# Moving the low part of two normed inputs by 64 bytes, the bias matmul to the third panel, and adding a narrow matmul: a float32 transformer kernel on one core

## What is computed

```
for i in range(2):
    h = h + mixer(rmsnorm(h, mix_norm[i]))          # layer 0: stick-breaking + hgrn2; layer 1: sliding window
    h = h + conv_glu_ffn(rmsnorm(h, ffn_norm[i]))   # up: 1024 -> 2 x 2816, 3-tap convolution, silu(gate)*up, down
    h = h + sigmoid(rmsnorm(h, ple_norm[i]) @ ple_gate[i]) * (p[i] @ ple_proj[i])
x = second_block(h, mem, ...)                       # three gated branches, an output matrix, a last norm
```

## Time and profile before

| | |
|---|---|
| median of 3 runs | 1003.98 us (1003.67 to 1004.08) |
| profiled execution, its own time | 1004.01 us |
| its span | 1002.1 us |
| granted clock of the PE | 1.0 in the whole span |
| PE busy | 984.9 us (98%) |
| PE weight loads busy | 883.2 us (88%) |
| DVE, ACT, POOL busy | 677.7, 573.5, 133.8 us |
| HBM read | 172.25 MB |

### The profile page before, as it was taken

One profiled execution on the slowest core, in us unless ns is written; L12 is line 12 of the kernel. 1 busy time (PEld: TensorE's weight loads), 2 busy tenths in 40 slices (PEclk: granted clock), 3 DMA queues, 4 the chain that ended last, 5 costly groups with the idle time before them and its releaser, 6 DMA issues.

```text
span 1002.1 us, 15515 instructions
## 1 busy us (share of the span) xinstructions
PE 984.9 (98%) x6218; PEld 883.2 (88%) x6218; DVE 677.7 (68%) x969; ACT 573.5 (57%) x801; POOL 133.8 (13%) x116
## 2 busy tenths in 40 slices
PE   8999999999999999999999999999999999999997
PEld 8998889999988888788999998888988889988886
DVE  5787577888864567886788886456564566854555
ACT  7747747656553576785756655356464465534433
POOL 4003202343310000000143331001000000000010
PEclk9999999999999999999999999999999999999999
DMA  9654256686555464336766655546635544466551
GB/s 310 207 170 126 84 146 178 197 250 195 185 195 184 167 210 168 126 103 171 198 172 182 194 172 203 177 166 205 211 127 169 168 149 146 142 197 205 175 172 56
DMA packets 159655, 174.33 MB, mean 174 GB/s; under 512 B 4126, under 2 KB 120336, under 8 KB 159584
## 3 DMA queue, kind: packets, MB, share of 16 engines
q1 hardware_dynamic: 157248, 167.65, 53.3%
q0 software_dynamic: 2160, 5.41, 1.7%
q10 hardware_dynamic: 176, 0.27, 0.1%
HBM read 172.25 MB, written 1.07 MB: 173 GB/s over the span
## 4 chain that ended last, share of the span: by engine, by line
PE 85%; ACT 6%; DVE 5%; issue 2%; DMA 1%; POOL 0%; POOLq 0%; ACTq 0%; DVEq 0%
PE bank L870 32%; PE bank L845 29%; PE bank L902 16%; PE bank L890 2%; ACT w_hi L1215 2%; PE bank L1004 1%; PE bank L930 1%; DVE w_lo L1541 1%; DMA w_raw<-in_ab_w_in 1%; ACT le L1325 1%; ACT L1325 1%; PE bank L950 0%; PE bank L973 0%; DVE le_s L1891 0%; ACT le_s L1465 0%
## 5 line engine op out<-in xcount | busy, mean ns | idle before, releaser
L1541 DVE TENSOR_TENSOR w_lo<-w_raw,w_hi 128x2048 fp32r<-128x2048 f32 x154 | 351.9, 2288 | 186.8 <-ACT w_hi L1215 186.6
L1215 ACT ACTIVATE w_hi<-w_raw 128x2048 fp32r<-128x2048 f32 x155 | 296.2, 1914 | 247.5 <-PE bank L870 114.2
L870 PE MATMUL bank<-x_hi,w_hi 128*128 128x256 f32 x720 | 205.9, 286 | 2.7 <-DVE w_lo L1541 1.8
L870 PE MATMUL bank<-x_lo,w_hi 128*128 128x256 f32 x720 | 203.7, 283 | 0.0
L870 PE MATMUL bank<-x_hi,w_lo 128*128 128x256 f32 x720 | 203.7, 283 | 0.0
L870 PEld LDWEIGHTS bank<-x_hi,w_hi 128*128 128x128 f32 x720 | 138.0, 192 | 4.4 <-DVE w_lo L1541 2.0
L845 PE MATMUL bank<-w_hi,x_hi 128*128 128x512 f32 x352 | 139.8, 397 | 1.0 <-DVE x_lo L1555 0.7
L870 PEld LDWEIGHTS bank<-x_lo,w_hi 128*128 128x128 f32 x720 | 138.1, 192 | 0.2
L870 PEld LDWEIGHTS bank<-x_hi,w_lo 128*128 128x128 f32 x720 | 138.0, 192 | 0.0
L845 PE MATMUL bank<-w_hi,x_lo 128*128 128x512 f32 x352 | 137.3, 390 | 0.0
L845 PE MATMUL bank<-w_lo,x_hi 128*128 128x512 f32 x352 | 137.1, 390 | 0.0
(11 more groups left out here) (344 smaller groups left out, 1471.6 us busy)
## 6 DMA issues: line engine op xcount, KB each, us to landing
w_raw<-in_ffn_up SPq DMA_DIRECT2D x88, 512.0 KB, 5.2
w_raw<-in_w_in SPq DMA_DIRECT2D x35, 1024.0 KB, 5.1
w_raw<-in_ffn_down SPq DMA_DIRECT2D x22, 1024.0 KB, 5.0
w_raw<-in_ab_w_in SPq DMA_DIRECT2D x13, 1024.0 KB, 5.4
w_raw<-in_ple_gate SPq DMA_DIRECT2D x8, 1024.0 KB, 5.1
w_raw<-in_c_w_in SPq DMA_DIRECT2D x6, 1024.0 KB, 5.3
w_raw<-in_ab_w_out SPq DMA_DIRECT2D x4, 1024.0 KB, 5.1
w_raw<-in_w_mem_kv SPq DMA_DIRECT2D x4, 1024.0 KB, 5.1
```

The costliest lines, as they stand in the source:

```text
L870: mm = pe.matmul(bank[b][:, c * 256:c * 256 + 256], wv[w][:, k, c * P:(c + 1) * P], x[:, k, :], start=(k == 0 and m == 0 and not (first an ...
L1215: act.activation(whi[n % RING][:, :], raw[n % RAW][:, :], ACT.Copy).then_inc(*mark("weights_hi", ("hi", n)))
L1541: dve.tensor_tensor(wlo[n % RING][:, :], raw[n % RAW][:, :], plain(whi[n % RING][:, :]), ALU.subtract).then_inc(*mark("weights_lo", ("lo", ...
```

## The change

`ODD = 64` names a second home for each low part, 64 bytes off a multiple of 128: `x_lo_odd` lies over `x_lo`, 64 bytes on, and `y_lo_odd` over `y_lo`, which itself now starts at a multiple of 128. Norms ffn0 and ffn1 use the odd homes, all others the even ones. So up0 stays odd; up1 goes from even to odd; kv, qs, wo1 and gate1 go from odd to even. For room behind `x_lo` 128 bytes are inserted, so that everything that is laid out after it (`h`, `y_hi`, `ident`, `vecs`, `g_hi`, `g_lo`, `pt_hi` and the rest) starts at 0 modulo 256 instead of 128, while the weights and `x_hi` stay where they were. `y_lo` starts at 128 modulo 256, both odd homes at 192. The `causal` mask moves into the table of vectors, whose convolution weights are no longer used then.

The bias step goes from the seventh panel of up0 to the third, and a narrow matmul of the same form (32 rows by 16 columns stationary, 128 moving, float32, from the identity, its result unused) is added before the third panel of up1.

```
-BIAS_AT = 6
+ODD = 64
+BIAS_AT = 2
...
+            if layer == 1 and i == BIAS_AT:
+                out.append(("narrow",))
             out.append(("panel", n))
...
+        XL_ODD = nc.alloc_sbuf_tensor_at("x_lo_odd", [P, KT, T], F32R, offset=top[0] - 4 * KT * T + ODD)
+        top[0] += 128
...
+        r.at = (r.at + 127) // 128 * 128
+        YL_ODD = nc.alloc_sbuf_tensor_at("y_lo_odd", [P, KT, T], F32R, offset=r.at + ODD)
         YL = r("y_lo", [P, KT, T], F32R)
+        r.at += ODD
...
-        causal = r("causal", [P, T])
+        causal = vflat[:, 3 * P:3 * P + T]
...
-        DEST.update({k: (YH, YL) for k in ("ffn0", "mix1", "ple1")})
+        DEST.update({k: (YH, YL) for k in ("mix1", "ple1")})
+        DEST["ffn0"], DEST["ffn1"] = (YH, YL_ODD), (XH, XL_ODD)
...
+                elif kind == "narrow":
+                    pe.wait_ge(*at(reader[3]))
+                    pe.matmul(bank[3][0:16, 0:P], ident[0:32, 0:16], ident[0:32, :], start=True, stop=True)
```

More of the change, by code:

```diff
@@ L776, in _ @@
                          bass.AP(tensor=io["b_spatial_2"].tensor, offset=0, ap=[[0, P], [1, GROUPS * P]]), "bsp")
-                    load(causal[:, :], io["c_causal"], "causal")
+                    load(causal, io["c_causal"], "causal")
                     load(small[:, 0:64], io["c_rope"], "rope")
```

## The result

The changed kernel takes 1005.7 us (median of 13 runs, 1005.24 to 1007.94), the kernel before 1003.98 beside it (13 runs, 1003.45 to 1005.8). The ratio is 1.0018, with a 95% interval of 1.001 to 1.0025. The forecast was 1000.8 us, and its range ended at 1003.2: it was wrong, on the wrong side of the kernel before. What came true is the main term of rival D, the slower `g` matmuls; D had a chance of 0.07 and a time of 1006.8.

The account below looks back on a forecast made before the run. The prediction took the PE's matmul pace as the bound (busy 984.9 of 1002.1 us). Gains of 1.19 (W stages), 0.42 (bias matmul) and 1.60 (up1) summed to 3.21 us, giving 1000.8 us, range 1000.0 to 1003.2.

Parts of the forecast that it names:

- rival D: The 128 inserted bytes slow every matmul reading `g`, and up0 loses its pace: +2.8 us, 1006.8 us; chance 0.07.
- W stages to the even home: In kv, qs, wo1 and gate1, the even home gains 1.19 us, bounds 0 and 1.45.
- The bias matmul at the third panel: In up0, four panels go from 5.760 to 5.654 us each, gaining 0.42 us.
- up1: Odd home with narrow matmul: 20 panels gain 2.13 us, the narrow matmul costs 0.53, net gain 1.60.
- The covers of the moved bias work: At up0's start, the bias row's copy, store and table loads stay hidden: 1.2 us to spare, costed at nothing.
- `g` and `pt`: Matmul groups reading `g` and `pt` stay unchanged at 389 ns, so nothing in the sum.
- needs a disturbance to fall into it: In up0 and up1, only the odd home has the fast pace, 5.654 us per panel, entered through a disturbance.
- B: Fast pace isn't found: in up1 alone 1002.9 us, chance 0.12; in up0 and up1 1004.9, chance 0.05.
- C: Something else of the Y pair, not the 64 bytes, sets the pace: 1004.1 or 1004.5 us; chance 0.06.
- E: The moved bias work collides with the start of up0, costing 1 to 2 us; chance 0.03.
- The 109.2 ns: The skill's gap for 256 columns at any address, set against the trace's 120.0 and 117.8 ns in up0.

Follow-up runs that it names:

- r1: The kernel before with only the 128 bytes inserted behind `x_lo`, the causal mask moved for room; 1010.2 us, ratio 1.0061.
- r2: The changed kernel with 256 bytes inserted instead of 128 and the even `y_lo` at 128 modulo 256; 1001.51 us, ratio 0.997.
- r11: The kernel before with the whole of its memory 128 bytes further on; 1003.0 us, ratio 0.9984.
- r5: r2 with `g_lo` alone at 0 modulo 256; 1005.15 us, one run.
- r3: r2 with the bias matmul back at up0's seventh panel and no narrow matmul; 1004.19 us, ratio 0.9994.
- r10: The kernel before with only the bias matmul moved from up0's seventh panel to its third; 1004.86 us, ratio 0.9998.
- r9: r7 with the bias matmul back at up0's seventh panel and no narrow matmul; 998.94 us, ratio 0.9941.
- r6: r2 with both parts of `g` at 192 modulo 256; 1005.8 us, one run.
- r4: The kernel before with only the narrow matmul added before up1's third panel, up1 staying in the even home; 1004.79 us, ratio 1.0003.
- r8: r2 with a second narrow matmul ahead of up1's ninth panel; 1002.85 us, one run.
- r7: r2 with separate homes for the high parts of norms ffn0 and ffn1, at 0 modulo 256 in up0 and up1; 999.39 us, ratio 0.9949.
- r12: r7 without the narrow matmul, the bias matmul staying at up0's third panel; 1000.53 us, ratio 0.9956.

## Why the prediction was wrong

The step that failed is in rival D: "within a tile the slices lie at multiples of 512 bytes, and a 64-byte effect suggests a period of 128". From the one step that a row showed, 64 bytes, I took the period, and put an unmeasured displacement of 128 bytes at a chance of 0.07. So the sum had `g` and `pt` at nothing, and the W stages at a gain. r1 shows that the 128 bytes by themselves cost 5.6 us (in the changed kernel `g` and `pt` took 4.39 us more), r2 that 256 bytes cost nothing, and r11 that what counts is the distance from the weights. The prediction itself said that no row shows such a pair. A part of a change that no row shows, and that touches the operand of the largest group, wanted a chance near that of the forecast.

Point by point:

- *W stages to the even home*, -1.19 forecast: +0.50 measured between the events of the table, some 0.7 with up1's first two panels taken out. The even home of `y_lo` is at 128, but `y_hi` had been moved to 0 beside it, and a step between the parts costs as much as a displacement of both (r5). With both at 128 (r3) the home gives 0.89; the step from one gate1 panel to 11.5 of such panels took 0.30 too much, all of it in kv, qs and wo1.
- *The bias matmul at the third panel*, -0.42: right as a part (r10: 0.43). In the changed kernel up0 gained 1.14, since its displaced `y_hi` gave it a third pace of 117.0 ns that no row of before had. It had this pace ahead of the bias matmul too, so the disturbance won nothing there. D said up0 would lose 1.59.
- *up1*, -1.60: -1.61. Each panel is at 5.654, and the narrow matmul's panel took 492.56 - 486.39 = 6.17, or 0.52 over that, against 0.53. That the number came out is in part luck: the forecast had the narrow matmul bring the fast pace, and in the changed kernel up1 had it without one. In r2 the step holds as it was forecast (120.0 ns before, 117.8 behind).
- *The covers of the moved bias work*: right. The copy of the bias row ended at 165.98 + 0.27 = 166.25, the store and the table loads that follow it cost nothing that shows, and all nineteen panels behind it average 5.618.
- *`g` and `pt`*, 0: +4.39, in the three stretches of the table. D had priced this at 2.8, with the 4.3 ns of an odd home; it was 5.7 ns per matmul, and the `pt` and other `g` matmuls count too.
- *Sum*: with r2's homes the forecast of -3.21 is met by -3.06. The part of the homes was read rightly from the profile; that the fast pace "needs a disturbance to fall into it" was not (r9, and the changed kernel itself), and the change as it was written had the 128 bytes in it besides.

Of the rivals, B didn't come true: up0 and up1 ran at the fast pace behind the disturbance in every kernel with the odd home that was disturbed once (after, r2, r10), though in the changed kernel they ran so ahead of it too. C is refuted by r3. E isn't seen.

The Trainium skill's rule that the PE never waits on anyone and reads moving data and weights through two independent ports ("SBUF — State Buffer", section "Who interferes with whom") leaves no room for what is measured: at one shape, one clock and one order of instructions, 226.7, 232.4 and 233.3 ns per matmul of 512 columns came from the distance between the operands (r2, r1, r6). The 109.2 ns that the prediction set against 120.0 were no fair test: the Trainium skill's "TensorE: Matmul & The Clock Gate", section "Back-to-back issue gap", gives N/2.4 + 2.5 ns for a matmul without its weight load, and every matmul here has one.

## What to carry to other kernels

Before inserting or aligning anything in a tuned kernel, list for every stage where its operands come to lie relative to the weights, and treat each distance that the trace of before doesn't hold as unpriced, above all for the largest group. Compare paces by the distance in time of the same event over many panels: 0.1 us per panel is plain there, while starts that differ by up to 1.9 us between executions (161.59 after, 163.45 in r10) hide gains under 1 us in the total. Look at the granted clock by the us before explaining such a difference. A placement that gains in one form of matmul can lose in another, so give each stage a home of its own, and check it with one kernel that has the homes alone. Read the pace on both sides of a matmul that is meant to change it.

## What the runs showed of the hardware

- The pace of back-to-back matmuls depends on the distance modulo 256 bytes between the weights and the two parts of the activation. For 512 moving columns it is 226.7 ns with both parts at the weights' place, 232.4 with both 128 bytes away (r1, after), 232.5 with the low part alone 128 away (r5), 233.3 with both 64 away (r6). In gate1 the first 72 matmuls add 0.31 us (4.3 ns each) with the low part alone 64 away (before), and 0.47 (6.5 ns each) with the high part alone 128 away (after).
- For 256 moving columns it is the other way round: equal places gave 120.0 ns and no other pace, even after a disturbance (r4). Unequal ones have two: 120.0 and 117.8 (before, r1, r3, r8), or 118.9 and 117.0 (r7, r9, r12).
- A small matmul of another form in between costs 0.5 us. It threw the PE out of the slow pace each time (before, r2, r8, r9), out of the fast one in r1 and r8, and not in the changed kernel (up0 and up1) and in up1 of r7. Without one, a pace held for all eighteen panels measured (r3, r9, r12).
- Behind the same idle stretch at 41 to 43 us the granted clock stays at 1.00 in some executions (before) and falls to 0.50 in others (r10), which moves all that follows by some 1.3 us.
- Why this is so stays open. No trace shows what the PE reads when, and whether 256 is the period for distances other than those tried, or for other shapes, wasn't tried.
